# Feed-forwards with the low part of the activations beside the high part: one 512-column matmul in place of two of 256

## What is computed

```
def rms_norm(x, w):
    y = xf * lax.rsqrt(jnp.mean(xf * xf, axis=-1, keepdims=True) + NORM_EPS)
    return (y * w.astype(jnp.float32)).astype(x.dtype)
def swiglu(x, w_gate, w_up, w_down):
    return (jax.nn.silu(x @ w_gate) * (x @ w_up)) @ w_down
...
    h = rms_norm(x, ffn1_norm[l])
    x = x + 0.5 * swiglu(h, ffn1_w_gate[l], ffn1_w_up[l], ffn1_w_down[l])
```

## Time and profile before

| | |
|---|---|
| median of three runs | 2407.28 us (2405.07 to 2407.91) |
| the profiled execution | 2407.24 us |
| its span, first to last instruction | 2405.4 us |
| granted TensorE clock, mean | 0.998 |
| PE, DVE, ACT, POOL busy | 99%, 67%, 50%, 15% of the span |
| feed-forward stages | a0 to 213, b0 445 to 639, a1 639 to 834, b1 1066 to 1262 us |

### The profile page before, as it was taken

The page is one execution under the profiler, slowest core; times in us unless marked ns, Lnnn a source line. Parts: engine busy times, 40 slices in busy tenths (PEclk is TensorE's granted clock), DMA queues, the critical chain, the costliest instruction groups (busy, mean ns, idle before and its releaser), DMA issues.

```text
span 2405.4 us, 40231 instructions
## 1 busy us (share of the span) xinstructions
PE 2371.5 (99%) x16977; PEld 2180.5 (91%) x16977; DVE 1607.8 (67%) x2416; ACT 1193.7 (50%) x1977; POOL 352.8 (15%) x382
## 2 busy tenths in 40 slices
PE   8999999999999999999999999999999999999998
PEld 7999889999999998999998768888889888889998
DVE  5676686877787677678866875755644655466753
ACT  5445666544444467555454653431433444555643
POOL 1311002323123100034430302000001000001000
PEclk9999999999999999999999999999999999999999
DMA  7768735676666684457773211455542433334652
GB/s 239 229 217 228 208 106 141 197 240 221 217 230 223 202 228 141 123 181 233 231 216 122 60 60 53 138 186 182 176 158 71 151 113 98 123 123 141 187 193 94
DMA packets 374113, 401.55 MB, mean 167 GB/s; under 512 B 44707, under 2 KB 346047, under 8 KB 373676
## 3 DMA queue, kind: packets, MB, share of 16 engines
q1 hardware_dynamic: 371160, 391.19, 51.7%
q10 hardware_dynamic: 2772, 7.78, 1.0%
HBM read 397.87 MB, written 4.22 MB: 167 GB/s over the span
## 4 chain that ended last, share of the span: by engine, by line
PE 82%; DVE 11%; ACT 3%; issue 1%; POOL 1%; SPq 1%; DMA 1%; DVEq 0%; ACTq 0%; POOLq 0%
PE bank L685 25%; PE bank L687 24%; PE bank L686 24%; DVE rounded L2480 4%; DVE plain L2455 2%; PE bank L693 2%; ACT rounded L1671 1%; PE bank L698 1%; PE bank L1109 1%; PE bank L1139 1%; DVE plain L2465 0%; DVE plain L2713 0%; PE bank L1310 0%; DVE plain L2753 0%; POOL plain L3547 0%
## 5 line engine op out<-in xcount | busy, mean ns | idle before, releaser
L685 PE MATMUL bank<-rounded 128*128 128x256 f32 (+2 forms) x3480 | 1079.6, 310 | 7.5 <-DVE rounded L2480 2.9
L686 PE MATMUL bank<-rounded 128*128 128x256 f32 (+2 forms) x3480 | 1065.4, 306 | 0.0
L687 PE MATMUL bank<-rounded 128*128 128x256 f32 (+2 forms) x3480 | 1065.3, 306 | 0.0
L2480 DVE TENSOR_TENSOR rounded<-plain,rounded 128x1024 fp32r<-128x1024 f32 (+1 forms) x630 | 736.8, 1216 | 407.6 <-ACT rounded L1671 407.3
L1671 ACT ACTIVATE rounded<-plain 128x1024 fp32r<-128x1024 f32 (+1 forms) x630 | 616.4, 1032 | 360.6 <-PE bank L687 266.4
L685 PEld LDWEIGHTS bank<-rounded 128*128 128x128 f32 x3480 | 665.4, 191 | 53.2 <-issue 9.9
L687 PEld LDWEIGHTS bank<-rounded 128*128 128x128 f32 x3480 | 665.6, 191 | 28.8
L686 PEld LDWEIGHTS bank<-rounded 128*128 128x128 f32 x3480 | 665.9, 191 | 27.9
L685 PE MATMUL bank<-rounded,rounded 128*128 128x256 f32 (+2 forms) x1472 | 449.0, 305 | 5.9 <-DVE rounded L2480 2.5
L687 PE MATMUL bank<-rounded,rounded 128*128 128x256 f32 (+2 forms) x1472 | 445.4, 303 | 0.0
L686 PE MATMUL bank<-rounded,rounded 128*128 128x256 f32 (+2 forms) x1472 | 445.3, 303 | 0.0
(11 more groups left out here) (316 smaller groups left out, 1856.2 us busy)
## 6 DMA issues: line engine op xcount, KB each, us to landing
plain<-in_mlp_w SPq DMA_DIRECT2D x64, 1024.0 KB, 5.3
plain<-in_ada_w SPq DMA_DIRECT2D x48, 1024.0 KB, 5.7
plain<-in_ffn_w_gate SPq DMA_DIRECT2D x44, 1024.0 KB, 5.9
plain<-in_ffn_w_up SPq DMA_DIRECT2D x44, 1024.0 KB, 5.7
plain<-in_ffn_w_down SPq DMA_DIRECT2D x32, 1024.0 KB, 5.6
plain<-in_w_in SPq DMA_DIRECT2D x32, 1024.0 KB, 5.5
plain<-in_od_w_in SPq DMA_DIRECT2D x32, 1024.0 KB, 5.3
plain<-in_ffn_w_down SPq DMA_DIRECT2D x16, 768.0 KB, 6.0
```

Of the source, the lines that this page charges most:

```text
L685: pe.matmul(dst, a[0], b[0], start=first and i == 0, stop=False)
L686: pe.matmul(dst, a[0], b[1], start=False, stop=False)
L687: ins = pe.matmul(dst, a[1], b[0], start=False, stop=last and i == n - 1)
L2480: dve.tensor_tensor(low, raw, top, SUB).then_inc(*done(("lo", m, half)))
```

## The change

1. *Operand.* The activations of a feed-forward are laid out as `HWr[:, k, 0, :]`, 512 words with high in the first 256 and low in the second (`hw(k)` gives the two). Blocks 0 to 4 use them as before in `product`.
2. *Whole operand.* In blocks 0 to 3 DVE makes x times gain times root for chunks 2 blk and 2 blk + 1 (`whole`), ACT its high part and POOL its low part, in `HWr[:, k, 1, :]`.
3. *Wide blocks.* From block 5 (`WIDE`) on, gate and up have two banks each, and `wide` moves 512 columns (high | low) under the high weights into the whole bank and 256 (high) under the low weights into columns 256 to 511. ACT copies columns 256 to 511 out, DVE adds columns 0 to 255; no multiplication by the root. ACT now does each step's copies, split, `fill`, and then silu or the high part.
4. *Third matrix.* Column blocks 0 to 2 use `wide` too, with hidden chunks laid out the same way (`hl`); DVE adds both halves of a bank to X in two instructions. Column block 3 is as before.
5. *adaLN.* `FOLDS`, `QUARTERS` and `SUMS` replace `TURNS`: the second vector's fold stands one step behind the first's, PE's small matmuls for it one step behind those for the first, and DVE's additions one step behind PE. In p0 folds stay. Two accumulators instead of four.

```diff
+def turns(behind):
...
-                out[s, step + (3 if step == 26 else 2) * v] = (u // 4, v)
+                out[s, step + behind + v] = (u // 4, v)
...
-TURNS = turns()
+FOLDS, QUARTERS, SUMS = turns(-2), turns(0), turns(1)
+WIDE = 5
...
+    def wide(dst, pairs, first=True, last=True):
+        n = len(pairs)
+        for i, (a, b) in enumerate(pairs):
+            pe.matmul(dst[:, 0:512], a[0], b, start=first and i == 0, stop=False)
+            ins = pe.matmul(dst[:, 256:512], a[1], b[:, 0:256], start=False, stop=last and i == n - 1)
+        return ins
...
         for blk in range(11):
+            if blk >= WIDE:
+                for kind, step in (("g", 2 * blk), ("u", 2 * blk + 1)):
+                    m = U[s, kind, blk]
+                    bs = [bank(s, kind, blk, j) for j in range(2)]
+                    ready(m)
+                    for k in range(8) if (blk, kind) == (WIDE, "g") else ():
+                        for x in new(at(s, "whole", k)):
+                            pe.wait_ge(*x)
+                    for j in range(2):
+                        keys = [("unit", m)] if j else []
+                        wide(bs[j], [(part(m, k, j * 128), M.HWr[:, k, 1, :]) for k in range(8)]).then_inc(
+                            *done((s, kind, blk, j), *keys))
+                    fill(s, step)
+                continue
...
-                    ins = product(bs[j][:, 0:256], [(part(m, k - k0, j * 128), (f.hr[:, k, :], f.lr[:, k, :]))],
-                                  k == 0, k == 21)
+                    if blk < 3:
+                        ins = wide(bs[j], [(part(m, k - k0, j * 128), f.hl[:, k, :])], k == 0, k == 21)
+                    else:
+                        ins = product(bs[j][:, 0:256], [(part(m, k - k0, j * 128), (f.hr[:, k, :], f.lr[:, k, :]))],
+                                      k == 0, k == 21)
...
+            if blk >= WIDE:
+                for kind, dst in (("g", lambda c: f.sg[:, c % 4, :]), ("u", lambda c: f.up[c % 4])):
+                    for j in range(2):
+                        c = 2 * blk + j
+                        for x in new(at(s, kind, blk, j), at(s, "hid", c - 4)):
+                            act.wait_ge(*x)
+                        act.activation(dst(c), M.bank(s, kind, blk, j)[:, 256:512], ACT.Copy, scale=1.0).then_inc(
+                            *done((s, kind, "rest", c)))
+                    hi(U[s, kind, blk] + 3)
+                    fill(s, 2 * blk + (kind == "u"))
...
+            for k in (2 * blk, 2 * blk + 1) if blk < 4 else ():
+                for x in new(at(s, "wholef", k)):
+                    act.wait_ge(*x)
+                act.activation(M.HWr[:, k, 1, 0:256], f.whole[:, k, :], ACT.Copy, scale=1.0).then_inc(*done((s, "wholehi", k)))
...
         if part == 3:
-            for v in vecs:
+            for v in vecs if n >= 7 else vecs[:1]:
                 folded(n, v)
...
-        if (s, step) in TURNS:
-            modulation(*TURNS[s, step])
+        if (s, step) in FOLDS and s != "p0" and FOLDS[s, step][1]:
+            folded(*FOLDS[s, step])
+        if (s, step) in SUMS:
+            modulation(*SUMS[s, step])
...
+            if blk >= WIDE:
+                for kind, dst in (("g", lambda c: f.sg[:, c % 4, :]), ("u", lambda c: f.up[c % 4])):
+                    for j in range(2):
+                        c = 2 * blk + j
+                        for x in new(at(s, kind, "rest", c)):
+                            dve.wait_ge(*x)
+                        dve.tensor_tensor(dst(c), M.bank(s, kind, blk, j)[:, 0:256], dst(c), ADD).then_inc(
+                            *done((s, kind, c), ("free", s, kind, blk, j)))
+                    lo(U[s, kind, blk] + 3)
+                    fill(s, 2 * blk + (kind == "u"))
+                continue
...
+                    if blk < 3:
+                        dve.scalar_tensor_tensor(X[:, o, 0:256], M.bank(s, "d", o)[:, 256:512], 0.5, X[:, o, 0:256], MUL,
+                                                 ADD).then_inc(*done())
```

53 lines of the change are left out of this document (41 added, 12 removed).

## The result

| | before | changed |
|---|---|---|
| median of 20 runs | 2406.99 us (2404.83 to 2409.43) | 2411.16 us (2407.92 to 2415.54) |
| span of the profiled execution | 2405.4 us | 2411.2 us |
| granted clock, mean | 0.998 | 0.996 |

The ratio is 1.0017, 95% interval 1.0011 to 1.0023: 4.2 us slower, a small difference but clear of noise. The forecast was 19 us faster, with a range up to 2396.

The account below looks back on a forecast made before the run. PE was taken as bound by each matmul's columns plus 13.3 ns. Terms 17.3 - 0.3 + 0.6 + 1.3 + 0.1 = 19.0 us, taken from 2407.2, gave 2388.2 us, range 2383 to 2396.

Parts of the forecast that it names:

- the term of the whole operand: Blocks 0 to 3: 8 operations each on DVE, ACT and POOL per feed-forward, ready before block 5; cost 0.
- the wide pair: Gates, ups and third matrix: a pair takes 346.7 ns instead of 360.0; 1296 pairs gain 17.3 us on PE.
- The 2.5 ns a matmul of the Trainium skill: Rule behind the third rival, saved matmul saves little: pairs gain 3.2 us, time 2402 to 2405; 4 in 100.
- Evictions in the wide blocks: Blocks 5 to 10: ACT copies low products out and DVE adds, ahead of ACT's next split; no new wait.
- the tight case: Unit behind an adaLN slice: split wanted after 5.55 us, ready by DVE at 4.5; 1 us left.
- The wait at the start of the third matrix: ACT splits d1 ahead of silu and block 10's high part; with a0's wait at 130.48, gain 1.3 us.
- Step 26: Third matrix of a0, b0, a1: old wait stays, about 0.8 us, losing 0.1 of the gain in each; -0.3 us.
- The late landing in a1: Step 26 of a1: wait was 1.3 us because weights landed late; d1's earlier split brings back 0.6 us.
- rival 1: The wait moves to ACT and DVE, copies standing ahead of the split in wide blocks: 2397.7 us; 9 in 100.
- Folds a step apart: Second fold (1.2 us) leaves the run of sums: -0.3 and +0.6 at step 26, +0.1 at step 11.
- the second: Rival: slower than before, each of 11 slices in wide blocks making PE wait for the split; 2410 us; 2 in 100.
- same: Measured outcome within about 0.2%, 4.8 us, of the kernel before; chance 0.03, against 0.95 faster and 0.02 slower.

Follow-up runs that it names:

- spaced: Changed kernel with the eight adaLN slices of b0 and a1 evenly four steps apart (2, 6, ... 30): 2401.08 us, 0.9969 of the kernel before.
- experiment 4: Also called no_whole: changed kernel without the whole operand, root left out of blocks 5 to 10: 2395.36 us, 0.9952 of the kernel before.
- experiment 7: Also called low_by_act: changed kernel with a plain copy by ACT replacing POOL's subtraction, low part left out: 2405.9 us, 0.9996 of the kernel before.
- fold_only: Changed kernel reduced to the adaLN part and new operand layout, no wide matmul, no whole operand: 2403.63 us, 0.9985 of the kernel before.
- gates_only: Changed kernel with the third matrix as before; adaLN part, whole operand and wide gates and ups kept: 2411.92 us, 1.0022 of the kernel before.
- high_behind: Changed kernel with whole operand begun in blocks 0 to 2, ACT's high part one block later behind the splits: 2406.66 us, 1.0001 of before.
- whole_fitted: As high_behind, but DVE subtracts instead of POOL, behind its evictions one block later: 2405.16 us, 0.9993 of the kernel before.
- experiments 8, 9 and 14: Wide gates and whole operand in a0 alone, grouped: 2398.77 us; changed kernel, no slice behind steps under 8: 2408.74; b0, a1 slices four steps apart: 2401.08.

## Why the prediction was wrong

**The step that failed** is the term of the whole operand, put at nothing: "They follow the evictions, and the last is done some 5 us after block 3; block 5 wants it a block later. Cost 0." I asked only whether the product would be ready for its reader. It was, barely: PE waits for it once, 1.2 us in b1. Even that part was counted too short. Timeline of the changed kernel, POOL, b0:

```profile
499.76 2.42 POOL L3638 TENSOR_TENSOR rounded<-plain,rounded 128x256 fp32r<-128x256 f32 x2
```

The last low part is done at 502.2, 11 us after block 3's last matmul (491.0) and not 5, and block 5 starts at 503.3. In spaced, where the other waits are gone, PE waits 1.3 us for it in three stages. But most of the cost was to whoever stands behind it. The 96 operations cost 15.8 us (experiment 4), mostly through DVE's queue: 5.1 us of delay gathered by step 11 of b0, passed on to evictions, silu and split, a 3.2 us wait of PE and a half clock behind it. The earlier trace rows already showed PE standing at this very place for 0.37 us: the path from DVE to PE had no room left before the change, in a stage where DVE is busy in 50.1 of 57 us. The price of an operation was also low: L2744 took 802 ns where I put 0.48 us, L3638 1419 where I put 1.07.

**Mis-sized**: the wide pair. The mechanism was right (starts alternate, 1296 matmuls are gone, both halves of the gain appear), but a 512-column step inside it takes 236 ns instead of 226.7 and the pair 353.2 instead of 346.7: 8.8 instead of 17.3 us. The row for 512 came from a stream of one width, and the mixed stream had no row. The pair of 346.7 does occur, in stretches of other runs (experiment 7), so this error is one of which pace a stream takes. The 2.5 ns a matmul of the Trainium skill (TensorE: Matmul & The Clock Gate, "Back-to-back issue gap"), which that section gives for a single matmul and not for a stream with a weight load before each, made 3.2 us in all. That is nearer to 8.8 than the forecast's 17.3, though a pair by it would take 325 ns and the trace has 353.2.

**Right, point by point.**
- Evictions in the wide blocks cost nothing in a0, b0 and a1, where the tight case behind a slice kept its room.
- The wait at the start of the third matrix went: d1 of b0 starts with 0.8 us to spare, and the 1.3 us of this term appear (experiment 4).
- Step 26 keeps its wait, 0.5 us between starts at its unit in the changed kernel. The late landing in a1 no longer tells: 0.5 us there too. It was forecast at 0.8.

**Wrong in smaller ways.**
- b1 shows rival 1 in small: two waits, 1.1 and 1.5 us between starts, at the ups of blocks 7 and 8, and 1.3 us of cost without the whole operand (experiment 4). The first has to do with prices: there the four sums took 5.82 us in no_whole and a split's two halves 3.38, where the tight case counts 4.87 and 2.36. The second is a bank: "DVE's addition a step behind PE, so it never waits for PE" leaves out that PE waits for DVE's addition, since it frees a bank.
- Folds a step apart were counted at 0.4 us (-0.3, +0.6, +0.1) and give 3.0, so this term was too small. The mechanism is the one named, the fold leaves the path; alone it clears the waits at steps 11 and 26 altogether (third matrix up to its last unit 59.84, 60.17 and 60.27 us in a0, b0 and a1 of fold_only), since neither the pace nor a second residual step eats the room there.
- Two slips of the working: rival 1 takes off half of the whole 19.0 us and not half of the wide units' gain (10.2 / 2 = 5.1 us), and 12 slices stand behind steps 10 to 21, not 11. Neither bears on the forecast.

Sum by measured parts: folds -3.0, third matrix -3.0, wide gates -5.2, whole operand +15.8: +4.6. That it comes near the measured +4.2 is no check, as each part is the difference of two neighbouring versions, and the sum is the changed kernel less before. The check is gates_only, which misses additivity by 2.3 us, and the stages: the traces of the changed kernel and of no_whole differ by 6.6, 6.9 and 2.7 us in b0, a1 and b1, 16.3 in all.

**Of the rivals** the second had the right sign and size (2410) but another mechanism: it put the loss on eleven slices in the wide blocks and on ACT's copies. The mechanism that decided, DVE's backlog in the blocks ahead of them, was none of the cases. By the forecast's own bound of 0.2% the result is "same", at 0.03. These 0.03 and the 0.02 on slower were too small for a change that gives an engine on a tight path 59 us more work.

**What stays open**: how the 10 us or more beside POOL's part divide between DVE's multiplication and ACT's high part; high_behind and whole_fitted moved several things at once, and neither operation was tried alone. Also open is why 512 columns take 229 to 236 ns in a feed-forward and 226.7 in p0, and what decides between pairs of 353.2 and of 346.9 ns in the same code. Putting DVE's addition back where it stood, which the bank wait of b1 asks for, was not tried. The rest of the account, that fewer slices in the early blocks leave room, was tried from both sides (experiments 8, 9 and 14).

## What to carry to other kernels

An operation off the critical path has two costs to check: whether its result is in time, and what it pushes back in its engine's queue. Where PE waits for that engine anywhere downstream, even for a third of a microsecond, the queue has no room left at that place, and delay gathered ahead of it reaches PE. Room has to be sought per block: a0, with no slice beside the same work, paid nothing. A buffer has a third cost: moving the operation that frees it later can stop whoever fills the next one. When a change adds work beside periodic work, re-space the periodic work with it: here the same eight slices four steps apart turned a loss of 4 us into a gain of 7.

## What the hardware showed that I had not expected

- After waits of PE of about 3.2 us the granted clock fell: 0.64 over the next 4.7 us, 512-column steps at 0.42 us, 1.6 and 2.7 us lost besides the wait. It fell after a wait of 2.3 us too, in a1 of low_by_act. Behind waits up to 1.5 us between starts in the same stages the units ran at full speed.
- One and the same stream of 512 and 256 columns in turn ran at two paces, 353.2 and 346.9 ns a pair, the second over twelve units on end in b0 of low_by_act. Grouped by width a pair took 349.4 ns.
- DVE's four sums of 128x1024 took 4.87 us alone and 6.5 to 6.8 beside POOL, and POOL's 128x256 subtraction 0.74 us on average in one group and 1.42 in another.
